# Last output projection of a two-block transformer kernel: first-half blocks without a barrier, second column half in two quarters

## The chip, the cores and the metric

One core of one Trainium2 chip. The metric is device time in microseconds (us) of one execution of the whole program; three executions of the kernel before took 3222.23, 3224.38 and 3224.39 us, median 3224.38. Engines: PE (TensorE, matmul) and PEld (its weight loads), DVE (VectorE), ACT (ScalarE), POOL (GpSimd), SP (SyncE, which issues the DMAs here).

## The reference

Two model blocks one after the other on x of 1024 tokens and 1024 channels, in float32. The first has a windowed attention mixer, a recurrent (LRU) mixer and two MLPs. The second, where the change lies, ends as follows (shortened):

```python
y_sb = stick_breaking_attention(...).reshape(B, S, SB_WIDTH) * jax.nn.silu(sb_g)
y_sw = sliding_window_sink_attention(...).reshape(B, S, SW_WIDTH) * jax.nn.silu(sw_g)
y = jnp.concatenate([y_sb, y_sw], axis=-1) @ w_out[l]
x = x + gate[:, None, :] * y
return rmsnorm(x, final_g)
```

So: an output projection 1024 x 1024, a gated residual, and an RMS norm over the channels of each token.

## The kernel before, in words

**Layout.** Activations lie transposed: channel n of a block of 128 on the partitions, tokens along the columns. X holds 8 such blocks of 128 x 1024. A "block" n of the output is 128 channels; "low" and "high" are the token columns 0 to 511 and 512 to 1023.

**Products in three parts.** Each float32 operand is split into a high part in fp32r (a copy by ACT) and the rest (a subtraction by DVE). A product is three matmuls: high x high, high x rest, rest x high. The activations' parts lie in H, the weights' in wsp.

**Weights.** `order` is a list written by hand of every weight block (128 x 1024, 512 KB) in the order of use. `load(b)` lets SP fetch block b into one of three buffers `raw`; `split(b)` has ACT copy it (wsp high) and DVE subtract (wsp rest), and then issues `load(b + 3)`. `piece(name)`, called as block b begins, splits blocks up to b + 2. The ACT copy of block b waits until TensorE is through with block b - 3.

**A projection.** `project` runs over output blocks: `take_pair` gives the next of four pairs of PSUM banks in turn, 8 x 3 matmuls of up to 512 columns go to it, and `evac` is called. The first matmul waits for `free` of both banks of the pair.

**The engines work in order.** `Queues.add` appends an instruction to one engine's list with the operations that it waits for; each engine works its list from the front. `Q.barrier()` puts a wait for the last operation of PE, ACT, DVE and POOL on each of these engines. Code lines of the profile are often a helper's: L283 `mm`, L138 `A` (an ACT activation), L141 `TT`, L144 `STT`, L149 `TS`, L415 the sum of squares in `Stats.add`, L399 the ACT table load, L66 a DMA issue.

**The end of the kernel.** The last attention (`attention_units` with `window_units`) has 16 units; between its steps TensorE gets pieces of other work in bank 7: eight gate jobs (`GateJob`) and the first four of the eight blocks of the out projection for the low columns (`OutJob`, in the order 0, 1, 6, 7). The attention also uses banks 0 to 6; its output of a unit leaves bank 6 by `out2`, whose parts go to H. `low_ready` names the operations that the low part of H depends on. `OutJob.leave` evacuates bank 7 by DVE (gated residual into X) and squares the result on ACT.

Then comes `Q.barrier()`, the ACT table load, and the loads of X blocks 2 to 5 from DRAM ("spill"), which wait for the barrier's operations. A first `project("out2", 4, ...)` computes the last four low blocks (2, 3, 4, 5), a second one the eight blocks of the high columns, 512 wide. `out_ev` evacuates a block: DVE adds gate x product to X, ACT squares it, DVE adds the square to a running sum (`Stats.add`; the first goes into the sum itself, the eighth into the total directly). After the second high block `root(0)` makes the low half's norm: `Stats.total` sums over the partitions on TensorE with a matrix of ones, then DVE, ACT (Ln, Exp) and three DVE operations (`finish`, `rsqrt`). From the fourth high block on each evacuation is followed by `final` of one low block: DVE multiplies X by the norm and SP writes 256 KB of output. After the last high block come the three low finals left, `root(1)` and eight finals of the high half.

```python
            for k in range(K):
                wh, wl, ready = piece(name)
...
                            op = mm(ps[:, c:c + m], w, r[:, c0 + c:c0 + c + m], k == 0 and i == 0, k == K - 1 and i == 2,
                                    ready, ops, *wait)
```

Of the kernel before, what the change touches and what calls it, by code (L numbers as in the profile page):

```python
# [10 lines left out]
ALU = mybir.AluOpType  # L11
# [102 lines left out]
def program(nc, D, out, stop=None, dbg=None):  # L114
    ctx = ExitStack()
    with ctx:
        def sb(name, shape, dt=F32):
            return ctx.enter_context(nc.sbuf_tensor(name, shape, dt))

        Q = Queues(nc, ctx)  # L120
# [10 lines left out]
        def dve(fn, *a):  # L131
            return Q.add("dve", fn, *a)
# [4 lines left out]
        def A(o, i, f, *a, **kw):  # L137
            return act(lambda e: e.activation(o, i, f, **kw), *a)  # L138
# [4 lines left out]
        def STT(o, x, s, y, op0, op1, *a):  # L143
            return dve(lambda e: e.scalar_tensor_tensor(out=o, in0=x, scalar=s, in1=y, op0=op0, op1=op1), *a)  # L144

        def TS(o, x, s1, s2, op0, op1, *a):
            if op1 is None:
                return dve(lambda e: e.tensor_scalar(o, x, s1, None, op0), *a)  # L148
            return dve(lambda e: e.tensor_scalar(o, x, s1, s2, op0, op1), *a)  # L149
# [4 lines left out]
        H = sb("H", [128, 2, 8, 1024], F32R)  # L154
# [13 lines left out]
        def place(off, shape, dt=F32):  # L168

            names[0] += 1  # L170
            with ExitStack() as st:
                if off:
                    st.enter_context(nc.sbuf_tensor(f"pad{names[0]}", [128, int(off) // 4], F32))
                return st.enter_context(nc.sbuf_tensor(f"p{names[0]}", shape, dt))

        def V(name, i=0, n=1):
            return vec[:, VEC[name] + i:VEC[name] + i + n]
# [7 lines left out]
        def blocks(name, idx, pieces=8):  # L185
            for i in idx:
                order.append((name, i, pieces))
# [29 lines left out]
        blocks("in2", (22, 23, 24, 25))  # L217
        blocks("in2", (22, 23, 24, 25))
        blocks("out2", (0, 1, 6, 7, 2, 3, 4, 5))
        blocks("out2", range(8))  # L220

        s_raw = [sem(f"s_raw{i}") for i in range(NR)]
# [23 lines left out]
        def piece(name):  # L246

            b, j = at
            assert order[b][0] == name, (order[b], name)
            if j == 0:  # L250
                for x in range(b + LA + 1):
                    split(x)
            return wsp[:, b % NS, 0, j * 128:(j + 1) * 128], wsp[:, b % NS, 1, j * 128:(j + 1) * 128], splits[b]

        def piece_done(op):
            b, j = at
            if j == order[b][2] - 1:
                uses[b] = [op]
                at[0], at[1] = b + 1, 0
            else:  # L260
                at[1] = j + 1
# [18 lines left out]
        X = place(0, [128, 8, 1024])  # L280

        def mm(o, l, r, start, stop, *a, **kw):
            return pe(lambda e: e.matmul(o, l, r, start=start, stop=stop, **kw), *a)  # L283
# [4 lines left out]
        def take_pair():  # L288
            p = pair[0]
            pair[0] = (p + 1) % 4  # L290
            return p

        def project(name, count, K, rhs, evac, N=1024, first=None, c0=0):
            later = first
            for n in range(count):
                p = take_pair()
                ps = PS[:, 2 * p:2 * p + 2, :].rearrange("p a b -> p (a b)")
                wait = [free[2 * p], free[2 * p + 1]]
                for k in range(K):
                    wh, wl, ready = piece(name)  # L300
                    rh, rl, ops = rhs(k)
                    for i, (w, r) in enumerate(((wh, rh), (wh, rl), (wl, rh))):
                        for c in range(0, N, 512):
                            m = min(512, N - c)
                            op = mm(ps[:, c:c + m], w, r[:, c0 + c:c0 + c + m], k == 0 and i == 0, k == K - 1 and i == 2,
                                    ready, ops, *wait)
                        wait = []
                    piece_done(op)
                if later:
                    later()  # L310
                fr, later = evac(n, p, ps[:, 0:N], op)
                free[2 * p] = free[2 * p + 1] = fr
            if later:
                later()
            return op
# [69 lines left out]
        Hops = [None] * 8  # L385
# [12 lines left out]
        def ln_exp():  # L398
            act(lambda e: e.preload_act_table_set("natural_log_exp_and_others"))  # L399
# [48 lines left out]
        def finish(st, R, M, y, t, N=1024):  # L448
            p, ps, o = st.total(N)
            m = TS(M, ps, 1.0 / 1024, eps_, ALU.mult, ALU.add, o)  # L450
            free[2 * p] = free[2 * p + 1] = [m]
            return rsqrt(R, y, t, M, m)
# [3 lines left out]
        def buf(off, N=1024):  # L456

            if (off, N) not in bufs:
                bufs[off, N] = place(off * KB, [128, N])
            return bufs[off, N][:, :]  # L460
# [161 lines left out]
        st = Stats(buf(80), [buf(84), buf(92)])  # L622
# [40 lines left out]
        for k in range(8):  # L663
            for j, p in enumerate(pairs):
                b = b0 + j
                rh, rl, ops = Hk(k)
                for i, (wi, r) in enumerate(((0, rh), (0, rl), (1, rh))):
                    for c in range(2):
                        op = mm(PS[:, 2 * p + c, :], wsp[:, b % NS, wi, k * 128:(k + 1) * 128], r[:, 512 * c:512 * c + 512],
                                k == 0 and i == 0, k == 7 and i == 2, splits[b], ops)  # L670
# [332 lines left out]
        ends = Q.barrier()  # L1003
# [29 lines left out]
        st = out_rest("out0", MOk, "mlp_norm0", xl0)  # L1033
# [6 lines left out]
        a = A(ct, V("c", 0, 8), ACT.Tanh, c_vec, scale=0.5)  # L1040
        o = STT(cond, ct, 1.0, V("c", 0, 8), ALU.add, ALU.mult, a)
# [142 lines left out]
        for n in range(8):  # L1184
# [23 lines left out]
            a = A(gq, gq, ACT.Tanh, L["gq"], scale=0.7978845608028654)  # L1208
# [12 lines left out]
        ends = Q.barrier()  # L1221
# [17 lines left out]
        st = out_rest("out1", MOk, "mlp_norm1", xl1)  # L1239
# [5 lines left out]
        o = STT(g2, modT[:, 8:16], 1.0, V("norm_g_2", 0, 8), ALU.add, ALU.mult, mod_ready)  # L1245
# [195 lines left out]
        for k in range(8):  # L1441
            o = STT(X[:, k, :], X[:, k, :], V("final_norm", k), R1, ALU.mult, ALU.mult, r1, Hops[k])
# [124 lines left out]
        for s in range(n_s + 3):  # L1567
# [17 lines left out]
            if 0 <= v < n_s:  # L1585
                c0, z, t, m, sh, sl, pb = view(v)
                o = A(m, m, ACT.Exp, F[v]["min"])
                o = A(m, m, ACT.Ln, o, bias=1.0)
                F[v]["m"] = STT(m, t, 0.125, m, ALU.mult, ALU.max, o)
            if s < n_s:  # L1590
                c0, z, t, m, sh, sl, pb = view(s)
                F[s]["zc"] = A(t, z, ACT.Copy, F[s]["qk"], got(s - 3, "pv"))
                free[ZB] = free[ZB + 1] = [F[s]["zc"]]
            if 0 <= u < n_s:
                c0, z, t, m, sh, sl, pb = view(u)
                F[u]["add"] = TT(t, t, pb, ALU.add, F[u]["cum"], F[u]["m"])
            if s < n_s:
                c0, z, t, m, sh, sl, pb = view(s)
                F[s]["min"] = TS(m, t, 0.125, 40.0, ALU.mult, ALU.min, F[s]["zc"], got(s - 2, "sl"), got(s - 2, "sh"))
            if 0 <= v < n_s:  # L1600
                c0, z, t, m, sh, sl, pb = view(v)
                F[v]["sh"] = A(sh, m, ACT.Copy, F[v]["m"], got(v - 2, "carry"))
                F[v]["sl"] = TT(sl, m, fz(sh), ALU.subtract, F[v]["sh"], got(v - 2, "carry"))
            if 0 <= u < n_s:
                c0, z, t, m, sh, sl, pb = view(u)
# [6 lines left out]
        ends = Q.barrier()  # L1612
# [10 lines left out]
        low, high = slice(0, 512), slice(512, 1024)  # L1623
        out_order = (0, 1, 6, 7, 2, 3, 4, 5)
        parts_of = [[None, None] for _ in range(8)]
        Hops[0:4] = [None] * 4
        st_low = Stats(buf(48)[:, low], [buf(52)[:, low], buf(52)[:, high]])
        st_high = Stats(buf(48)[:, high], [buf(96)[:, low], buf(96)[:, high]])
        after_gates = [None, None]

        class GateJob:
# [43 lines left out]
        def low_ready(k):  # L1675
            return parts_of[k][0] if k < 4 else [o for n in range(4) for o in parts_of[4 + n][0]]
# [31 lines left out]
        def left():  # L1708
            return bool(now["job"] or gates_left or outs_left)
# [41 lines left out]
                        dict(dve=ahead_dve, fill=ahead_fill, end=finish_now))  # L1751
        leave_now()
        assert not left() and not now["half"]
        ends = Q.barrier()
        ln_exp()
        for k in range(2, 6):
            xl3[k] = Q.dma(None, X[:, k, :], D["spill"][:, k, :], sp2[k], *ends)
        for f in sums:
            f()
        Hops[:] = [None] * 8  # L1760
        s_out = sem("s_out")
        fin = [dict(st=st_low), dict(st=st_high)]

        def root(hf):
            cs = slice(512 * hf, 512 * hf + 512)
            fin[hf]["r"] = finish(fin[hf]["st"], buf(72)[:, cs], buf(64)[:, cs], buf(76)[:, cs], buf(68)[:, cs], 512)

        def final(k, hf):
            x = X[:, k, 512 * hf:512 * hf + 512]
            o = STT(x, x, V("final_g_2", k), buf(72)[:, 512 * hf:512 * hf + 512], ALU.mult, ALU.mult, fin[hf]["r"])  # L1770
            return Q.dma(s_out, out[:, k, 512 * hf:512 * hf + 512], x, o)

        def out_ev(hf, at_n, x, p, ps, op):
            n = at_n[x]
            cs = (low, high)[hf]
            o = STT(X[:, n, cs], ps, modT[:, 16 + n:17 + n], X[:, n, cs], ALU.mult, ALU.add, op, xl3[n])
            fin[hf]["st"].add(8 - len(at_n) + x, X[:, n, cs], o)
            if hf and x == 1:
                root(0)
            if hf and x > 2:  # L1780
                final(x - 3, 0)
            return [o], None

        project("out2", 4, 8, Hk, lambda *a: out_ev(0, out_order[4:], *a), N=512)
        project("out2", 8, 8, Hk, lambda *a: out_ev(1, range(8), *a), N=512, c0=512)
        for k in range(5, 8):
            final(k, 0)
        root(1)
        for k in range(8):
            od = final(k, 1)  # L1790
        Q.add("sp", None, od, *sp1, *sp2, *mk_sp)
        assert at[0] == len(order), (at, len(order))
        block = ctx.enter_context(nc.Block())
# [128 lines left out]
```

How the kernel before makes its waits and increments, by code:

```python
            def run(eng):  # L93
                seen = {}
                for o in self.q[name]:
                    for d in o.deps:
                        if seen.get(d.sem.name, 0) < d.val:
                            eng.wait_ge(d.sem, d.val)
                            seen[d.sem.name] = d.val
                    if o.fn is None:
                        continue
                    ins = o.fn(eng)
                    if o.sem is not None:
                        ins.then_inc(o.sem, 1 if o.sem is self.sems.get(name) else 16)
```

## Time and profile before

| | |
|---|---|
| three executions | 3222.23, 3224.38, 3224.39 us |
| the profiled execution | 3220.72 us |
| its span, first to last instruction | 3218.9 us |
| mean granted TensorE clock | 0.987 |
| instructions | 34594 |
| HBM read, written | 170.63 MB, 14.68 MB |

The times in rows of the trace are microseconds from the start of the span, in the profiled execution. That execution is 3.66 us under the median of the three. A row of the timeline gives start, length, engine, line, operation, what it writes and reads, its size, and in brackets how long the engine stood idle before it and what ended that. The length of an instruction contains some latency: the next one on the same engine may start a little before its end.

### The profile page before, as it was taken

To read this page: it belongs to the slowest core of one execution; us is meant where nothing else is said; L and a number is where in the kernel's file an instruction comes from. 1 tells how busy PE (TensorE), PEld (TensorE's weight loads), DVE (VectorE), ACT (ScalarE), POOL (GpSimd) and SP (SyncE) were. 2 spreads that over 40 slices of the span, in tenths; PEclk is the share of its full clock that TensorE was granted. 3 is DMA by queue.
4 is the path that set the end of the run, shared out by engine and by line. 5 is a ranking of instruction groups with operands and counts; after the bars stand their busy time and mean duration, and the time that the engine had idled before them with its cause. 6 is when DMAs were issued, how large, how long until landed. Compare 5 with 4: busy or idle time off the path is not lost. (4 is left out here: it accounts for less than half of the span.)

```text
span 3218.9 us, 34594 instructions
## 1 busy us (share of the span) xinstructions
PE 3087.8 (96%) x14272; PEld 2391.5 (74%) x14272; DVE 1689.7 (52%) x2159; ACT 1099.7 (34%) x1711; POOL 89.9 (3%) x70
## 2 busy tenths in 40 slices
PE   8999999999999999999979999999999999999898
PEld 7884567788888888877767888888887686665566
DVE  7737854644444433589743633333334734566575
ACT  4215632311111111388622311111111515776452
POOL 0004510000000000000000000000000000000000
PEclk9999999999999999999989999999999999999999
DMA  4420011122222211211121111111111131000213
GB/s 148 116 90 1 1 73 40 58 68 72 71 66 78 73 46 53 75 47 43 59 85 40 45 48 46 46 51 48 46 46 46 53 124 33 20 20 14 92 53 111
DMA packets 53933, 188.86 MB, mean 59 GB/s; under 512 B 6224, under 2 KB 6608, under 8 KB 53648
## 3 DMA queue, kind: packets, MB, share of 16 engines
q1 hardware_dynamic: 53776, 186.65, 17.6%
q8 instruction: 113, 1.85, 0.2%
q14 instruction: 44, 0.36, 0.0%
HBM read 170.63 MB, written 14.68 MB: 58 GB/s over the span
## 5 line engine op out<-in xcount | busy, mean ns | idle before, releaser
L283 PE MATMUL PS<-H,wsp 128*128 128x512 f32 x6864 | 1612.0, 394 | 40.2 <-DVE wsp L141 17.0
L283 PEld LDWEIGHTS PS<-H,wsp 128*128 128x128 f32 x6864 | 1290.9, 189 | 344.9 <-issue 32.0
L283 PE MATMUL PS<-p,wsp 128*128 128x512 f32 (+1 forms) x3840 | 895.4, 393 | 20.7 <-DVE p L141 20.7
L283 PEld LDWEIGHTS PS<-p,wsp 128*128 128x128 f32 x3840 | 711.5, 189 | 198.6 <-ACT wsp L138 21.5
L138 ACT ACTIVATE p<-p 128x1024 f32<-128x1024 f32 (+7 forms) x426 | 361.0, 872 | 860.9 <-DVE p L144 680.0
L138 ACT ACTIVATE wsp<-raw 128x1024 fp32r<-128x1024 f32 (+1 forms) x263 | 272.6, 1040 | 703.4 <-PE PS L283 492.4
L141 DVE TENSOR_TENSOR p<-p,PS 128x1024 f32<-128x1024 f32 (+2 forms) x232 | 244.4, 1053 | 501.4 <-PE PS L283 501.2
L141 DVE TENSOR_TENSOR wsp<-raw,wsp 128x1024 fp32r<-128x1024 f32 (+1 forms) x263 | 316.9, 1207 | 162.0 <-ACT wsp L138 156.5
L141 DVE TENSOR_TENSOR p<-PS,p 128x1024 f32<-128x1024 f32 (+1 forms) x114 | 130.7, 1147 | 380.1 <-PE PS L283 355.9
L141 DVE TENSOR_TENSOR p<-p 128x1024 fp32r<-128x1024 f32 (+5 forms) x239 | 239.6, 1010 | 115.3 <-ACT p L138 112.1
L283 PE MATMUL PS<-p 128*64 128x256 f32 (+9 forms) x1432 | 284.9, 463 | 13.7 <-DMA p<-mk_dram 4.8
L144 DVE SCALAR_TENSOR_TENSOR p<-p 128x1024 f32<-128x1024 f32 (+3 forms) x197 | 209.5, 1070 | 68.4 <-ACT p L138 64.8
L138 ACT ACTIVATE p<-PS,sm 128x256 f32<-128x256 f32 (+2 forms) x256 | 127.9, 508 | 231.8 <-DVE sm L148 139.8
L138 ACT ACTIVATE p<-PS 128x512 f32<-128x512 f32 (+4 forms) x198 | 121.2, 639 | 221.7 <-PE PS L283 198.7
L283 PEld LDWEIGHTS PS<-p 128*64 128x64 f32 (+2 forms) x1432 | 123.8, 167 | 97.1 <-issue 55.4
L535 PE MATMUL PS<-cf,p 128*128 128x128 f32 x600 | 89.5, 284 | 23.4 <-DVE p L148 9.9
L498 DVE TENSOR_REDUCE sm<-PS 128x2 f32<-128x768 f32 (+3 forms) x96 | 94.7, 987 | 26.3 <-PE PS L283 25.9
L535 PEld LDWEIGHTS PS<-cf,p 128*128 128x128 f32 x600 | 67.2, 144 | 52.8 <-issue 14.9
L526 POOL TENSOR_SCALAR p<-p,sm 128x384 f32<-128x384 f32 (+1 forms) x64 | 87.8, 1373 | 250.2 <-DVE sm L519 250.2
L283 PE MATMUL PS<-p,triR 128*128 128x512 f32 (+3 forms) x352 | 79.4, 359 | 15.4 <-DVE p L141 14.6
L283 PE MATMUL PS<-wsp,H 128*128 128x256 f32 (+2 forms) x576 | 88.8, 316 | 0.0
L283 PEld LDWEIGHTS PS<-wsp,H 128*128 128x128 f32 x576 | 80.8, 190 | 7.8
(70 smaller groups left out, 1054.3 us busy)
## 6 DMA issues: line engine op xcount, KB each, us to landing
raw<-in_in_dram SPq DMA_DIRECT2D x70, 512.0 KB, 3.5
raw<-in_dn_dram SPq DMA_DIRECT2D x65, 512.0 KB, 3.5
raw<-in_up_dram SPq DMA_DIRECT2D x64, 512.0 KB, 3.5
raw<-in_out_dram SPq DMA_DIRECT2D x40, 512.0 KB, 3.5
p<-in_ada_dram SPq DMA_DIRECT2D x24, 512.0 KB, 4.4
p<-in_x_dram SPq DMA_DIRECT2D x16, 512.0 KB, 7.8
raw<-in_kv_dram SPq DMA_DIRECT2D x16, 512.0 KB, 3.5
spill_dram<-p SPq DMA_DIRECT2D x16, 512.0 KB, 3.0
```

What stands on the lines that cost most here:

```text
L138: return act(lambda e: e.activation(o, i, f, **kw), *a)
L141: return dve(lambda e: e.tensor_tensor(o, x, y, op), *a)
L144: return dve(lambda e: e.scalar_tensor_tensor(out=o, in0=x, scalar=s, in1=y, op0=op0, op1=op1), *a)
L283: return pe(lambda e: e.matmul(o, l, r, start=start, stop=stop, **kw), *a)
L498: o = dve(lambda e: e.tensor_reduce(mx, S, AX.X, ALU.max), op, prev)
L526: last[1] = pool(lambda e, P_=P_, r=r: e.tensor_scalar(P_, P_, r, None, ALU.mult), o)
L535: o = pe(lambda e, t_out=t_out, t_in=t_in: e.transpose(t_out, t_in, ident), probs[J * u + j], free[b])
```

## The change

The last projection's first-half blocks are issued with no barrier before them and wait for the parts of H (`low_ready`); the DMAs that waited on the barrier wait on the last operations of PE, ACT and DVE. The high half is computed in two passes over all eight weight blocks, for the columns 512 to 767 and 768 to 1023. The weight blocks of `out2` stand once more in `order`. There are three sets of column statistics, roots and finals: the low half (512 columns) and the two quarters (256 each). The root of a set is made after the second block of the next pass; its finals follow the fourth to eighth evacuation of that pass, in groups of 2, 2, 2, 1 and 1.

```diff
         blocks("out2", (0, 1, 6, 7, 2, 3, 4, 5))
+        blocks("out2", range(8))
         blocks("out2", range(8))
...
-        st_high = Stats(buf(48)[:, high], [buf(96)[:, low], buf(96)[:, high]])
+        spans = (low, slice(512, 768), slice(768, 1024))
+        st_high = [Stats(buf(48)[:, spans[1 + i]], [buf(96)[:, 512 * i + 256 * j:512 * i + 256 * j + 256] for j in range(2)])
+                   for i in range(2)]
...
-        ends = Q.barrier()
+        ends = [Q.last("pe"), Q.last("act"), Q.last("dve")]
         ln_exp()
         for k in range(2, 6):
             xl3[k] = Q.dma(None, X[:, k, :], D["spill"][:, k, :], sp2[k], *ends)
         for f in sums:
             f()
-        Hops[:] = [None] * 8
+        def high_ready(k):
+            return parts_of[k][1] if k < 4 else [o for n in range(4) for o in parts_of[4 + n][1]]
+
         s_out = sem("s_out")
-        fin = [dict(st=st_low), dict(st=st_high)]
...
+        fin = [dict(st=st) for st in (st_low, *st_high)]
+
+        def root(x):
+            cs = spans[x]
+            fin[x]["r"] = finish(fin[x]["st"], buf(72)[:, cs], buf(64)[:, cs], buf(76)[:, cs], buf(68)[:, cs],
+                                 cs.stop - cs.start)
+
+        def final(k, x):
+            cs = spans[x]
+            o = STT(X[:, k, cs], X[:, k, cs], V("final_g_2", k), buf(72)[:, cs], ALU.mult, ALU.mult, fin[x]["r"])
+            return Q.dma(s_out, out[:, k, cs], X[:, k, cs], o)
+
+        def out_ev(x, at_n, i, p, ps, op):
+            n, cs = at_n[i], spans[x]
             o = STT(X[:, n, cs], ps, modT[:, 16 + n:17 + n], X[:, n, cs], ALU.mult, ALU.add, op, xl3[n])
-            fin[hf]["st"].add(8 - len(at_n) + x, X[:, n, cs], o)
-            if hf and x == 1:
-                root(0)
-            if hf and x > 2:
-                final(x - 3, 0)
+            fin[x]["st"].add(8 - len(at_n) + i, X[:, n, cs], o)
+            if x and i == 1:
+                root(x - 1)
+            if x and i > 2:
+                for k in ((0, 1), (2, 3), (4, 5), (6,), (7,))[i - 3]:
+                    final(k, x - 1)
             return [o], None
 
-        project("out2", 4, 8, Hk, lambda *a: out_ev(0, out_order[4:], *a), N=512)
-        project("out2", 8, 8, Hk, lambda *a: out_ev(1, range(8), *a), N=512, c0=512)
-        for k in range(5, 8):
-            final(k, 0)
-        root(1)
+        project("out2", 4, 8, lambda k: (H[:, 0, k, :], H[:, 1, k, :], low_ready(k)),
+                lambda *a: out_ev(0, out_order[4:], *a), N=512)
+        for x in (1, 2):
+            project("out2", 8, 8, lambda k: (H[:, 0, k, :], H[:, 1, k, :], high_ready(k)),
+                    lambda *a: out_ev(x, range(8), *a), N=256, c0=spans[x].start)
+        root(2)
         for k in range(8):
-            od = final(k, 1)
+            od = final(k, 2)
```

## Rows read from the trace of the kernel before

**Rows 1.** The page: busy us, share of the span and instructions of each engine

```profile
PE 3087.8 (96%) x14272; PEld 2391.5 (74%) x14272; DVE 1689.7 (52%) x2159; ACT 1099.7 (34%) x1711; POOL 89.9 (3%) x70
```

**Rows 2.** The chain of waits, 3130 us to the end: start, length (us), what

```profile
3130.62 0.70 DVE p L144
...
3132.70 0.67 DVE p L144
...
3133.39 0.64 ACT p L138
...
3134.12 68.92 PE PS L283 x292
```

**Rows 3.** Timeline of TensorE, 3126 us to the end

```profile
3129.48 1.08 PE L283 MATMUL PS<-p 128*64 128x256 f32 x8
3134.12 34.50 PE L283 MATMUL PS<-H,wsp 128*128 128x512 f32 x144 [3.55 <-ACT p L138]
3168.46 1.88 PE L283 MATMUL PS<-p,cf 128*128 128x512 f32 x4
...
3204.62 1.96 PE L283 MATMUL PS<-p,cf 128*128 128x512 f32 x4 [1.60 <-ACT p L138]
```

**Rows 4.** Timeline of DVE and ACT in the last projection

```profile
3141.45 0.75 DVE L144 SCALAR_TENSOR_TENSOR p<-PS,modT,p 128x512 f32<-128x512 f32 x1 [3.75 <-PE PS L283]
...
3146.89 0.75 DVE L144 SCALAR_TENSOR_TENSOR p<-PS,modT,p 128x512 f32<-128x512 f32 x1 [1.81 <-PE PS L283]
3147.68 0.63 ACT L138 ACTIVATE p<-p 128x512 f32<-128x512 f32 x1 [3.86 <-DVE p L144]
3148.22 1.04 ACT L138 ACTIVATE wsp<-raw 128x1024 fp32r<-128x1024 f32 x1
...
3149.29 1.22 DVE L141 TENSOR_TENSOR wsp<-raw,wsp 128x1024 fp32r<-128x1024 f32 x1 [0.26 <-ACT wsp L138]
...
3157.77 0.75 DVE L144 SCALAR_TENSOR_TENSOR p<-PS,modT,p 128x512 f32<-128x512 f32 x1 [1.81 <-PE PS L283]
...
3174.83 1.22 DVE L141 TENSOR_TENSOR wsp<-raw,wsp 128x1024 fp32r<-128x1024 f32 x1
3175.97 0.74 DVE L144 SCALAR_TENSOR_TENSOR p<-PS,modT,p 128x512 f32<-128x512 f32 x1
```

**Rows 5.** TensorE's timeline, and windows: us, busy PE PEld DVE ACT POOL, PEclk, DMA, GB/s

```profile
3136.00:3138.00 2.00, 2.00 (x7) 1.59 (x6) 1.23 (x1) 0.45 (x1) 0.00 (x0) 0.61 0.98 393
...
3010.72 0.40 PE L283 MATMUL PS<-p,cb 128*128 128x128 bf16 x4 [1.84 <-ACT p L138]
...
3011.00:3013.00 2.00, 2.00 (x8) 1.58 (x7) 1.02 (x3) 0.93 (x5) 0.00 (x0) 0.57 0.57 141
...
3121.73 3.02 PE L283 MATMUL PS<-H,wsp 128*128 128x512 f32 x12 [1.66 <-DVE p L144]
...
3122.00:3123.00 1.00, 1.00 (x6) 0.78 (x6) 0.93 (x5) 1.00 (x3) 0.00 (x0) 1.00 0.00 0
```

**Rows 6.** Groups by shape on TensorE, columns 256: busy us, mean ns

```profile
L283 PE MATMUL PS<-p,wsp 128*128 128x256 f32 x192 | 23.4, 281 | 0.0
L283 PE MATMUL PS<-p,cf 128*128 128x256 f32 x4 | 1.0, 379 | 0.0
```

**Rows 7.** Groups by shape on DVE and ACT, 256 columns: busy us, mean ns

```profile
L144 DVE SCALAR_TENSOR_TENSOR p<-p 128x256 f32<-128x256 f32 x10 | 4.2, 422 | 4.0 <-ACT p L138 3.9
L144 DVE SCALAR_TENSOR_TENSOR p<-p,vec 128x256 f32<-128x256 f32 x8 | 3.8, 480 | 0.0
...
L138 ACT ACTIVATE p<-p 128x256 f32<-128x256 f32 x34 | 13.8, 411 | 10.7 <-DVE p L149 9.4 <-DVE p L415 0.9
```

**Rows 8.** Timeline of DVE: the eight final products at the end

```profile
3210.84 5.39 DVE L144 SCALAR_TENSOR_TENSOR p<-p,vec 128x512 f32<-128x512 f32 x8
```

**Rows 9.** DMA issues from 3100 us on: count, KB each, median us to landing

```profile
raw<-in_out_dram SPq DMA_DIRECT2D x10, 512.0 KB, 3.5
out_dram<-p SPq DMA_DIRECT2D x16, 256.0 KB, 2.1
```

More of the change, by code:

```diff
@@ L1759, in program @@
             f()
-        Hops[:] = [None] * 8
+        def high_ready(k):
+            return parts_of[k][1] if k < 4 else [o for n in range(4) for o in parts_of[4 + n][1]]
         s_out = sem("s_out")
-        fin = [dict(st=st_low), dict(st=st_high)]
[L1764 to L1771, printed above, removed]
@@ L1773, in out_ev @@
-        def out_ev(hf, at_n, x, p, ps, op):
-            n = at_n[x]
-            cs = (low, high)[hf]
-            o = STT(X[:, n, cs], ps, modT[:, 16 + n:17 + n], X[:, n, cs], ALU.mult, ALU.add, op, xl3[n])
-            fin[hf]["st"].add(8 - len(at_n) + x, X[:, n, cs], o)
-            if hf and x == 1:
-                root(0)
-            if hf and x > 2:
-                final(x - 3, 0)
-            return [o], None
-        project("out2", 4, 8, Hk, lambda *a: out_ev(0, out_order[4:], *a), N=512)
```

## The prediction

> **What bounds the kernel now.** I read the page first: TensorE's share of the span [rows 1]. TensorE is busy 96% of the time, so the only questions are where it stands still and how long the kernel runs after its last product. Next the chain of waits over the last 90 us [rows 2]. It goes through the last attention unit (DVE, ACT, DVE, DVE, ACT one after the other from 3130.62), then one unbroken piece of TensorE work of 68.92 us, then the tail: evacuation, square, column total, root, eight final products, output. Then TensorE's timeline of that stretch [rows 3]: it ends the attention at 3130.56, stands still 3.55 us, runs 144 products (four blocks of the first column half are 96, the rest are the second half) and a column total of 1.88 us; the last total starts after 1.6 us without work at 3204.62. Last, one step of DVE and ACT in this stretch [rows 4]: both have spare time, DVE's evacuation and subtraction take 2.0 us of a block of 5.44.
>
> So there are two places to gain, the gap at 3130.56 and the tail behind TensorE's piece, which ends at 3203.04 [rows 2]. TensorE's rate pays for everything between.
>
> **1. The barrier.** Without it the first block left (out2 number 4) needs its weights (split since 3123), its H parts (long done) and its PSUM pair. That last one decides. `take_pair` hands out the pairs in turn; counting its calls from the start of the program, 319 come before this block's, and 319 mod 4 is 3. Pair 3 is banks 6 and 7. Bank 7 is freed by the evacuation of the last block computed inside the attention, the DVE instruction that the chain shows from 3132.70 to 3133.37 [rows 2]. TensorE can start at about 3133.40 in place of 3134.12: **-0.72 us**, not 3.55. ACT's table load, the next weight copy and the spill loads that SP issues still wait for the square that ends at 3134.03. The new dependences of the spill loads name the same last operations, so they land as before. They are first needed when block 4 ends, after 3140, and are not late. No engine is queued behind anything new.
>
> **2. The clock.** After the 3.55 us gap the granted clock fell to half (1.2 GHz of 2.4); the first block's evacuation came 7.33 us after its start (3141.45) [rows 4], 1.7 over 5.44 and 0.17 of latency; the window of 3136 shows 0.61 [rows 5]. The new gap is 2.84 us. The trace has a shorter one that led to the same fall, 1.84 us before 3010.72 (granted clock 0.57 from 3011), while 1.66 us before 3121.73 did not (1.00 from 3122 on) [rows 5]. By these rows I keep the loss: 0. The Trainium skill, "TensorE: Matmul & The Clock Gate", section "HAM oscillation", asks for a gap longer than the new one before the clock drops; by it the clock would stay up here, and the 1.84 us row disagrees with it. By that rule the sum would be 1.7 us lower.
>
> **3. Products of half the width.** The second half is 8 blocks of 24 products of 512 columns, 5.44 us a block (evacuations at 3146.89 and, two blocks on, 3157.77 [rows 4]), 43.5 us. It becomes 16 blocks of 24 products of 256 columns. A group of 192 with this shape took 23.4 us [rows 6], 0.122 us each, 2.93 us a block, 46.8 us: **+3.3 us** at TensorE's pace. The column total of the first quarter is new on TensorE's queue: half of 1.88 us, **+0.95 us** (four narrow total products took 1.0 [rows 6]).
>
> **4. Weights twice.** Eight more blocks mean eight more SP loads of 512 KB, ACT copies of 1.05 us and DVE subtractions of 1.22 us. The block in front of them is now 2.93 us, not 5.44, and it is here that the cover goes. DVE and ACT work in order and wait for one another in a ring: evacuation (DVE), square (ACT), weight copy (ACT, queued behind the square), subtraction (DVE), next evacuation. At 512 columns the offsets are 0.79 to the square, 0.54 to the copy, 1.07 to the subtraction, and 1.14 from a subtraction to the next evacuation (3174.83 to 3175.97) [rows 4]: 3.54 us, well under 5.44. At 256 columns, with 0.48 for an operation with a vector operand, 0.42 without, 0.41 on ACT [rows 7], 0.03 for a handover, and 0.06 to 0.08 less between independent neighbours (products 0.75 long stand 0.67 apart [rows 8]): 0.51 + 0.33 + 1.08 + 1.14 = **3.06 us, over TensorE's 2.93**. With the other work DVE has in a step:
> - two 512-wide final products (0.67 each, eight took 5.39): 0.95 to the sum of squares, 0.36 for it, 1.35, 1.14 = 3.80 us, three steps; with one, 3.12, and once, beside the last block, 3.06;
> - the 512-wide root: 1.31, 0.72, ACT 0.66 + 0.66, DVE 0.72 + 0.72 + 0.69, 1.14 = 6.62 us;
> - the 256-wide root: 1.31, 0.45, 0.44 + 0.44, 0.46 + 0.45 + 0.42, 1.14 = 5.11 us;
> - two 256-wide final products (0.42 each): 3.29 us.
>
> The look-ahead of two blocks hides some of the lag, then it is used up. From the last evacuation of the first half, 3157.77 - 0.72 = 3157.05: 3.54 + 3.06 + 6.62 + 3.06 + 3 x 3.80 + 3.12 + 3.06 (first quarter), + 3.06 + 5.11 + 3.06 + 2 x 3.29 (second, to its sixth evacuation) = 3208.7. From there on DVE has no weights left to split: 3.29 - 1.14, then 0.95 + 0.36 + 0.42 (one final left in front) put the last evacuation at **3212.6**. TensorE, which could begin its last block when the last subtraction ended at 3208.8, is through at 3212.0, a little sooner. Against 3203.07: **+9.5 us**. By TensorE's pace alone it would be -0.72 + 3.3 + 0.95 = +3.5; the other 6 us is DVE's lag.
>
> **5. The tail.** Before, the last evacuation starts 0.03 us behind TensorE's piece, at 3203.07, and the eighth final product ends at 3216.23 [rows 8]: 13.16 us. At 256 columns: evacuation 0.51, square 0.44, total 1.08, mean 0.45, two ACT steps 0.88, three DVE steps 1.36, eight finals 7 x 0.42 + 0.48 = 8.1, with the small waits 8.2: **-5.0 us**. The last write is 128 KB, not 256; it lands 2.1 us after issue now [rows 9]. The new one I put 0.3 us sooner; bounds 0 and 0.8, what a write that starts before the engines are full could save.
>
> **Sum:** +9.5 - 5.0 - 0.3 = **+4.2 us**. The profiled execution took 3220.72 us, its span 3218.9, so 3224.9 on its scale. It is 3.7 under the median of the runs, and I add the change to the median: 3224.38 + 4.2 = 3228.6, written as **3228.5**.
>
> **Loads.** A raw buffer is loaded after its subtraction and wanted by the copy three blocks on, about 7 us later at the new rhythm; landing takes 3.5 us [rows 9]. Final writes of 512 KB a step now run beside them, together about 300 GB/s; the window of 3136 shows 393 GB/s [rows 5]. I cost it at 0. The cover is gone if landing passes 7 us.
>
> **The rivals.**
> A, the forecast: DVE's ring sets the pace of both quarters. Own range 3226.5 to 3231, chance 0.50.
> B, the same, but the granted clock does not fall after the shorter gap: -1.7, 3226.8. For it: the gap shrank by a fifth. Against it: the 1.84 us row. Chance 0.15. (The rule of the Trainium skill named under 2 points to this one.)
> C, DVE keeps up (the square and the copy overlap more than in rows 4, or narrow operations are cheaper than rows 7), TensorE sets the pace: +3.5 - 5.0 - 0.3 = -1.8, 3222.6. Against it: DVE's own work in a step with two finals is 0.42 + 0.36 + 1.35 + 1.14 = 3.3, over 2.93 with no wait at all. Chance 0.12.
> D, slower: weight loads come late. Its place is the stretch in which first-quarter finals, 256 KB each, go out between weight loads on the one SP queue. It decides from a landing time of 7 us; at 9 us three-block cycles last 9 + 2.3 in place of some 10, and over the quarters 4.6 us are added (3233.1), at 10 us 7.6 (3236). For it: writes and loads share the DMA engines, and in the window of 3136 these are full (share 0.98) [rows 5]. Chance 0.18.
> E, the bank is another and TensorE starts at 3130.6: -2.8 on A, with the clock kept -4.5, 3224.0 to 3225.7. That is the change doing what it says in full. Chance 0.05.
>
> **How the numbers follow.** 0.2% is 6.4 us, about what a measurement of this kernel can tell from no change. Faster by more needs C and E together with the clock kept (-1.8 - 2.8 - 1.7 = -6.3), and the error of the medians on top: 0.03. Slower by more: D, and the top of A if the clock also falls once at the narrow root: 0.24. The rest, 0.73, is within. Range: from C, 3222.5, to the lower part of D, 3233.5.
>
> **What would show it.** Right: TensorE's restart after the attention about 0.7 us sooner with an idle time of 2.8 us; matmuls of 256 columns at 0.122 us each; TensorE idle on DVE's weight subtraction, 4 to 6 us in all, in the stretch from about 3170; DVE without idle time on TensorE there; last evacuation near 3212.6; tail of 8.2 us. Wrong: a restart near 3130.6, no TensorE idle time behind the subtraction (C), or idle time in front of ACT's weight copy, ended by a load (D). A time under 3220 or over 3236 would break the whole account.

## The result, and the profile after

The changed kernel took 3228.71 us in the median of 19 executions, the kernel before 3222.23 us in 19 beside them. The two medians are 6.5 us apart, 0.20%. The ratio with its interval, 1.0015 with 95% within 1.0008 to 1.0022, puts the change lower: 2.6 to 7.1 us slower, 4.8 at the middle (the means of the 19 are 4.7 apart). The forecast was +4.2 us.

The two profiled executions differ by more, 3218.9 and 3227.0 us. 3.7 us of that lie ahead of anything the change touches: the last attention product ends at 3130.57 in the one and 3134.24 in the other, with the same instructions up to there and the granted clock falling at other places (from 86 to 94 us, for one, it is 1.00 before and 0.79 in the changed kernel). So the traces are compared from the end of the last attention product on. I call the time from there to the end of the span the **stretch**: 88.3 us before, 92.7 us after, **+4.4 us**.

Engine totals on the page of the changed kernel hardly show it: 9 us more on TensorE, 12 on DVE.

```profile
span 3227.0 us, 35088 instructions
...
PE 3097.1 (96%) x14468; PEld 2406.5 (75%) x14468; DVE 1702.1 (53%) x2193; ACT 1108.5 (34%) x1729; POOL 89.7 (3%) x70
```

TensorE's timeline answers to [rows 3].

```profile
3133.16 1.08 PE L284 MATMUL PS<-p 128*64 128x256 f32 x8
3137.18 29.39 PE L284 MATMUL PS<-H,wsp 128*128 128x512 f32 x144 [2.94 <-DVE p L144]
3166.40 1.88 PE L284 MATMUL PS<-p,cf 128*128 128x512 f32 x4
3167.72 6.31 PE L284 MATMUL PS<-H,wsp 128*128 128x256 f32 x48
3174.23 6.16 PE L284 MATMUL PS<-H,wsp 128*128 128x256 f32 x48 [0.20 <-DVE wsp L141]
3181.05 3.11 PE L284 MATMUL PS<-H,wsp 128*128 128x256 f32 x24 [0.66 <-DVE wsp L141]
...
3202.86 12.62 PE L284 MATMUL PS<-H,wsp 128*128 128x256 f32 x96 [1.45 <-DVE wsp L141]
3217.01 1.10 PE L284 MATMUL PS<-p,cf 128*128 128x256 f32 x4 [1.53 <-ACT p L138]
```

Before, TensorE stood still 3.55 us for ACT, which came through the barrier; now it stands still 2.94 us for one DVE instruction, the evacuation of bank 7. And inside the quarters there is idle time that the kernel before did not have: five waits for DVE's weight subtraction. The view of the waits from 3135 on sums TensorE's (us in total, times, longest):

```profile
PE PS L284 <- DVE wsp L141: 3.6, 5, 1.5
PE PS L284 <- DVE p L144: 2.9, 1, 2.9
PE PS L284 <- ACT p L138: 1.5, 1, 1.5
```

The ring of DVE and ACT, timeline of both, to set beside [rows 4]: one plain step from 3174.00, then one with two finals from 3177.06.

```profile
3174.00 0.48 DVE L144 SCALAR_TENSOR_TENSOR p<-PS,modT,p 128x256 f32<-128x256 f32 x1
...
3174.51 0.42 ACT L138 ACTIVATE p<-p 128x256 f32<-128x256 f32 x1 [2.79 <-DVE p L144]
3174.83 1.05 ACT L138 ACTIVATE wsp<-raw 128x1024 fp32r<-128x1024 f32 x1
3174.96 0.42 DVE L416 TENSOR_TENSOR p<-p 128x256 f32<-128x256 f32 x1 [0.49 <-ACT p L138]
3175.91 1.23 DVE L141 TENSOR_TENSOR wsp<-raw,wsp 128x1024 fp32r<-128x1024 f32 x1 [0.53 <-ACT wsp L138]
3177.06 0.48 DVE L144 SCALAR_TENSOR_TENSOR p<-PS,modT,p 128x256 f32<-128x256 f32 x1
...
3178.36 1.41 DVE L144 SCALAR_TENSOR_TENSOR p<-p,vec 128x512 f32<-128x512 f32 x2
...
3179.69 1.22 DVE L141 TENSOR_TENSOR wsp<-raw,wsp 128x1024 fp32r<-128x1024 f32 x1
3180.82 0.48 DVE L144 SCALAR_TENSOR_TENSOR p<-PS,modT,p 128x256 f32<-128x256 f32 x1
```

The plain step is 3.06 us (3174.00 to 3177.06), the other 3.76. No evacuation here has idle time of DVE in front of it that a TensorE product ended: TensorE's results are ready, and it is DVE that is late. In the plain step DVE itself is idle for 0.49 and 0.53 us, both times for ACT. That is the ring.

The end of the kernel, DVE's timeline (compare [rows 8]) and the DMA issues from 3160 on (compare [rows 9]):

```profile
3215.94 0.48 DVE L144 SCALAR_TENSOR_TENSOR p<-PS,modT,p 128x256 f32<-128x256 f32 x1
...
3220.89 3.26 DVE L144 SCALAR_TENSOR_TENSOR p<-p,vec 128x256 f32<-128x256 f32 x8
```

```profile
raw<-in_out_dram SPq DMA_DIRECT2D x11, 512.0 KB, 3.6
out_dram<-p SPq DMA_DIRECT2D x8, 256.0 KB, 2.8
out_dram<-p SPq DMA_DIRECT2D x16, 128.0 KB, 1.8
```

### The profile page after: what moved, and what is told of

It reads as the page before. It is cut to its first block and busy times, and to the rows that moved or that the text cites. A ratio compares the mean times of both kernels' runs of the same rounds, so it can differ in the third digit from the quotient of the medians.

```text
span 3227.0 us, 35088 instructions
## 1 busy us (share of the span) xinstructions
PE 3097.1 (96%) x14468; PEld 2406.5 (75%) x14468; DVE 1702.1 (53%) x2193; ACT 1108.5 (34%) x1729; POOL 89.7 (3%) x70
## 5 line engine op out<-in xcount | busy, mean ns | idle before, releaser
L284 PE MATMUL PS<-H,wsp 128*128 128x512 f32 (+1 forms) x7056 | 1619.5, 389 | 43.1 <-DVE wsp L141 20.1
L138 ACT ACTIVATE wsp<-raw 128x1024 fp32r<-128x1024 f32 (+1 forms) x271 | 280.9, 1040 | 705.0 <-PE PS L284 492.4
L141 DVE TENSOR_TENSOR wsp<-raw,wsp 128x1024 fp32r<-128x1024 f32 (+1 forms) x271 | 326.6, 1207 | 164.6 <-ACT wsp L138 159.2
L527 POOL TENSOR_SCALAR p<-p,sm 128x384 f32<-128x384 f32 (+1 forms) x64 | 87.7, 1371 | 251.2 <-DVE sm L520 251.2
```

Of the source, the lines that this page charges most:

```text
L141: return dve(lambda e: e.tensor_tensor(o, x, y, op), *a)
L527: last[1] = pool(lambda e, P_=P_, r=r: e.tensor_scalar(P_, P_, r, None, ALU.mult), o)
```

## The experiments

The theory is the forecast's: bank 7 holds back the restart, and in the quarters the order of work in the queues of DVE and ACT, not TensorE, sets the pace. The rivals are the full gain of the barrier, late loads, and the price of narrow products. Every kernel was profiled; where a ratio stands, it was also timed over 11 executions (the changed kernel over 19) beside the kernel before. Rows with one execution rest on their trace alone. The columns that I compare:

| kernel | idle before restart | last evacuation | stretch | ratio to before (95%) |
|---|---|---|---|---|
| before | 3.55 | 72.5 | 88.3 | |
| changed | 2.94 | 81.7 | 92.7 | 1.0015 (1.0008 to 1.0022) |
| barrier_only | 2.94 | 71.9 | 87.7 | 0.9999 (0.999 to 1.0008) |
| quarters_only | 3.55 | 82.2 | 93.2 | 1.0012 (1.0003 to 1.0021) |
| after_next_pair | none | 77.1 | 88.1 | 1.0002 (0.9993 to 1.0012) |
| after_no_sub | 2.94 | 75.3 | 86.3 | one execution |
| width_only | 3.55 | 75.0 | 90.8 | one execution |
| after_ring_open | 2.94 | 75.2 | 86.3 | one execution |
| halves_next_pair | none | 67.4 | 83.1 | 0.9982 (0.9973 to 0.9991) |
| ring_open_next_pair | none | 70.7 | 81.7 | 0.9982 (0.9973 to 0.9992) |

Times in us; the last evacuation is counted, like the stretch, from the end of the last attention product. "None" means that TensorE's row there shows no idle time.

**barrier_only** takes one part of the change alone.

```diff
-        ends = Q.barrier()
+        ends = [Q.last("pe"), Q.last("act"), Q.last("dve")]
...
-        project("out2", 4, 8, Hk, ...)
-        project("out2", 8, 8, Hk, ..., N=512, c0=512)
+        project("out2", 4, 8, lambda k: (H[:, 0, k, :], H[:, 1, k, :], low_ready(k)), ...)
+        project("out2", 8, 8, lambda k: (H[:, 0, k, :], H[:, 1, k, :], high_ready(k)), ..., N=512, c0=512)
```

> The kernel before with the barrier alone taken out (blocks wait for their parts of H), the second half still 512 wide. The stretch counted is from the end of the last attention product to the end of the span: 88.3 us before, 92.8 us in the changed kernel. Theory (the first block left waits for bank 7): TensorE stands still 2.9 us in place of 3.55, the stretch is 87.7, and the time is 0.6 us lower, which no median can show. Rival (the barrier was worth its whole gap): idle time under 0.3 us and a stretch of 84.8 or less.

Stretch 87.7, as the theory has it; TensorE's timeline names the same waited-for instruction as in the changed kernel:

```profile
3124.77 1.08 PE L283 MATMUL PS<-p 128*64 128x256 f32 x8
3128.79 34.51 PE L283 MATMUL PS<-H,wsp 128*128 128x512 f32 x144 [2.94 <-DVE p L144]
```

The barrier was worth 0.6 us, because another wait ended 0.6 us before it. That is read from the traces; the ratio can't tell 0.6 us from nothing.

**quarters_only** is the changed kernel with the barrier back (the first two lines above, the other way round).

> The changed kernel with the barrier put back: the two quarters alone. Theory: all of the loss is the quarters'; stretch 93.4 us (92.8 + 0.6), time 5 us over the kernel before. Rival (taking out the barrier let other work collide and made part of the loss): stretch under 92.8.

93.2, and a ratio clear of 1. The two parts add: -0.6 and +4.9 make the change's 4.4 to within 0.1. The quarters are the whole loss.

**after_next_pair** tests that it is the bank.

```diff
+        take_pair()
         project("out2", 4, 8, lambda k: (H[:, 0, k, :], H[:, 1, k, :], low_ready(k)),
```

> The changed kernel with one pair of banks skipped ahead of the remaining first-half blocks, so that the first of them gets banks 0 and 1 and the fourth gets 6 and 7. Theory: TensorE goes on without standing still (under 0.3 us in place of 2.94), the granted clock stays at full, the first block takes 5.6 us to its evacuation instead of 7.35, and the stretch falls from 92.8 by 2.9 + 1.7 = 4.6 to 88.2, level with the kernel before. The first evacuation can be late by a spill load that lands after it. Rival (another wait stands right behind the bank, the spill loads or the weight split): idle time stays over 2 us and the stretch over 91. Second rival (DVE sets the pace so firmly that the earlier start is lost again): evacuations of the quarters come no earlier than in the changed kernel, counted from the end of the attention.

```profile
3128.84 1.08 PE L284 MATMUL PS<-p 128*64 128x256 f32 x8
3129.86 27.84 PE L284 MATMUL PS<-H,wsp 128*128 128x512 f32 x144
3157.54 1.88 PE L284 MATMUL PS<-p,cf 128*128 128x512 f32 x4
```

No idle time, and 144 products take 27.84 us in place of 29.39. The granted clock (the value after the five engines in the window rows) is 1.00 after the restart here and fell to 0.50, the lower level, in the changed kernel:

```profile
3139.00:3141.00 2.00, 2.00 (x6) 1.58 (x5) 0.90 (x1) 1.06 (x1) 0.00 (x0) 0.50 0.82 285
...
3130.00:3140.00 10.00, 10.00 (x44) 8.22 (x45) 5.79 (x8) 5.19 (x6) 0.00 (x0) 1.00 0.56 204
```

The stretch is 88.1 for 88.2 expected; the last evacuation moved by 4.6 us, the same amount as the restart and the clock together, so the second rival falls too. One skipped pair is worth seven times what the removed barrier was. The first block's evacuation came at 7.3 us after the attention, not 5.6, which the expectation had allowed for: the block needs X from a spill load, which now lands later than the product and a weight subtraction that stands ahead of it on DVE (3135.79 to 3137.02; the last 0.18 us before the evacuation at 3137.19 are a wait for that load). The second block's came at 11.2 all the same; TensorE's row above has no idle time from it.

**after_no_sub** takes DVE's work away.

```diff
             o1 = A(h, src, ACT.Copy, loads[b], uses.get(b - NS), splits.get(b - NS))
-            o2 = TT(l, src, fz(h), ALU.subtract, o1, uses.get(b - NS), loads[b], splits.get(b - NS))
+            if b >= len(order) - 16:
+                o2 = o1
+            else:
+                o2 = TT(l, src, fz(h), ALU.subtract, o1, uses.get(b - NS), loads[b], splits.get(b - NS))
```

> The changed kernel without the DVE subtraction that makes the low part of the weights, for the last 16 blocks of weights (both quarters); it leaves out that part of the computation, and the products with the low part read what an earlier block left there. Theory (the ring of DVE and ACT sets the pace): with 1.22 us less on DVE in each step TensorE sets the pace again; its idle time on weights in the quarters goes from 3.6 us to 0, evacuations stand 2.95 us apart, and the last evacuation, 81.7 us after the end of the attention in the changed kernel and 72.5 in the one before, comes at about 76 (72.5 + 3.3 + 0.95 - 0.6). Rival (loads of weights or the width of the products set the pace): last evacuation stays over 80.

TensorE's wait for weights is gone, and the quarters run in unbroken pieces:

```profile
3167.18 23.59 PE L287 MATMUL PS<-H,wsp 128*128 128x256 f32 x192
3190.62 1.02 PE L287 MATMUL PS<-p,cf 128*128 128x256 f32 x4
3191.29 17.62 PE L287 MATMUL PS<-H,wsp 128*128 128x256 f32 x144
```

The last evacuation comes at 75.3 (76 expected), and with DVE free the evacuations stand 2.88 us apart. All widths are as in the changed kernel, so they did not set its pace. The loads are the same in number and size, but not in time: a raw buffer is free here after the copy, without waiting for a subtraction, so its next load can go out sooner. That late loads were not the cause is shown by the changed kernel's own trace, in which no weight copy of the last projection waits for a load. DVE set the pace; but whether by how much it has to do or by its order this run can't tell.

**after_ring_open** takes nothing away. `split` is cut in two, and `out_ev` hands the next weight copy to ACT ahead of the square, and the subtraction to DVE ahead of the sum of squares and the root; the finals come ahead of the subtraction.

```diff
...
             o = STT(X[:, n, cs], ps, modT[:, 16 + n:17 + n], X[:, n, cs], ALU.mult, ALU.add, op, xl3[n])
-            fin[x]["st"].add(8 - len(at_n) + i, X[:, n, cs], o)
-            if x and i == 1:
-                root(x - 1)
+            nb = at[0] + LA
+            c = split_high(nb)
             if x and i > 2:
                 for k in ((0, 1), (2, 3), (4, 5), (6,), (7,))[i - 3]:
                     final(k, x - 1)
+            split(nb, c)
+            fin[x]["st"].add(8 - len(at_n) + i, X[:, n, cs], o)
+            if x and i == 1:
+                root(x - 1)
             return [o], None
```

> The changed kernel with the opened ring alone (no pair skipped). Theory: gap of 2.9 us and half clock as in the changed kernel, last evacuation at about 75.3 us after the end of the attention (as in the run without the subtraction) in place of 81.7, stretch 86.3 in place of 92.7. Rival (the ring is only part of the lag): last evacuation over 78.

TensorE's timeline has no wait for weights left:

```profile
3163.30 23.59 PE L292 MATMUL PS<-H,wsp 128*128 128x256 f32 x192
...
3187.41 17.62 PE L292 MATMUL PS<-H,wsp 128*128 128x256 f32 x144
```

Last evacuation at 75.2, the same as without the subtraction (75.3): 6.5 us came back by order alone. The edit moves the copy, the subtraction and the finals together; what each move is worth was not tried. The rival that DVE has too much work is wrong on the whole, though it does fall behind in the steps with two 512-wide finals. DVE's timeline of such a step, in ring_open_next_pair, which has the same order:

```profile
3170.43 0.48 DVE L144 SCALAR_TENSOR_TENSOR p<-PS,modT,p 128x256 f32<-128x256 f32 x1
3170.82 1.41 DVE L144 SCALAR_TENSOR_TENSOR p<-p,vec 128x512 f32<-128x512 f32 x2
3172.14 1.22 DVE L141 TENSOR_TENSOR wsp<-raw,wsp 128x1024 fp32r<-128x1024 f32 x1
3173.28 0.42 DVE L424 TENSOR_TENSOR p<-p 128x256 f32<-128x256 f32 x1
3173.61 0.48 DVE L144 SCALAR_TENSOR_TENSOR p<-PS,modT,p 128x256 f32<-128x256 f32 x1
```

3.18 us a step with no idle time, 0.3 over TensorE's 2.88, in three steps; the look-ahead of two blocks covers that. In the changed kernel the same work took 3.76.

**width_only** is the kernel before with each weight tile in wsp used for two products of 256 columns in place of one of 512.

```diff
...
-                        for c in range(0, N, 512):
-                            m = min(512, N - c)
-                            op = mm(ps[:, c:c + m], w, r[:, c0 + c:c0 + c + m], k == 0 and i == 0, k == K - 1 and i == 2,
+                        for c in range(0, N, 256 if two else 512):
+                            m = min(256 if two else 512, N - c)
+                            op = mm(PS[:, 2 * p + c // 256, 0:256] if two else ps[:, c:c + m], w,
+                                    r[:, c0 + c:c0 + c + m], k == 0 and i == 0, k == K - 1 and i == 2,
```

> The kernel before with the second half's products cut to 256 columns, two beside each other for each weight tile, in the two banks of the pair; every weight block is still used once. It measures the width alone. From the run without the subtraction: 2.88 us for 24 narrow products, so 5.76 a block in place of 5.44 and 5.34, the last evacuation 2.6 to 3.4 us later than 72.5, at 75.5, and the stretch 91.3. Rival (narrow products cost more only when each brings new weights): under 73.5. With the barrier in place, gap 3.55 us.

Blocks of the second half stand 5.76 us apart, twice 2.88, and the last evacuation is 2.5 us later than before. So narrow products cost the same whether or not each weight block is fetched and split for its 256 columns alone. What the run does not separate is the load of the tile into TensorE: that still goes with every product, 487 loads by the rows in place of 288.

```profile
L283 PEld LDWEIGHTS PS<-H,wsp 128*128 128x128 f32 x487 | 66.8, 194 | 9.0 <-issue 4.5
```

Whether the extra time is that of the loads or of the shorter products stays open. The 2.5 us are the plain price of the narrow products on TensorE. The new column total adds 0.85: in the run without the subtraction, the two blocks around it end 6.61 us apart (3190.82 to 3197.43), where 5.76 are products. That is 3.4 us in all.

**halves_next_pair** and **ring_open_next_pair** ask what of it beats both kernels. The first is barrier_only with `take_pair()`; the second is after_ring_open with `take_pair()`.

> The kernel before without the barrier, with one pair of banks skipped ahead of the remaining first-half blocks; the second half 512 wide in one pass. If gap, clock and quarters simply add: the stretch from the end of the last attention product to the end of the span is 87.7 (barrier alone out) less the 2.9 us gap and the 1.6 us of half clock = 83.1 us, 5.2 under the kernel before. Rival (the earlier start is given back where the spill loads or the tail end last): 86 or more.

> The changed kernel with the skipped pair, and with the ring of DVE and ACT opened: after each evacuation the next weight copy comes ahead of the square on ACT, and the subtraction ahead of the sum of squares and the root on DVE. No operation is added or left out. Theory (it is the order in the two queues, not DVE's amount of work, that makes the quarters slow): TensorE waits for weights 0.3 us at most in place of 3.6, evacuations come 2.88 us apart, the last one 70.7 us after the end of the attention in place of 77.1, and the stretch is 81.8 us against 88.1 with the skipped pair alone. Rival (DVE has too much to do in the steps with two 512-wide finals, 3.3 us of its own work in 2.9): TensorE still waits 2 us or more and the stretch stays over 84.

Both come out as added up, 83.1 and 81.7, and both are faster than the kernel before, ratio 0.9982, with intervals that end under 1. TensorE's waits in ring_open_next_pair from 3130 on are a single row, the square before the last column total:

```profile
PE PS L292 <- ACT p L138: 1.1, 1, 1.1
```

By the traces the quarters with the ring open are 1.4 us ahead of the halves: 3.3 us more up to the last evacuation, 4.7 us less from there to the end. The timed medians (3216.43 and 3217.93 us) agree in sign, but the two intervals are nearly the same, so the times don't show it.

The next limit is already to be seen there. The view of the tile raw in ring_open_next_pair, from 3160 on, has the weight copy waiting for loads, which happened nowhere in the last projection of the changed kernel:

```profile
  DMA raw<-in_out_dram: 5.1, 4
...
DMA to landing us min/median/max: 3.4/4.4/5.8
```

TensorE did not feel it yet.

## Why the prediction was right, point by point

The change and its mechanism were right; that the time itself, 3228.5 us, came within 0.2 us of 3228.71 is luck. The forecast stood on a median of three executions, 3224.38; over 19 the kernel before has 3222.23, and the 2.15 us too many there made up for the 2.3 us by which the two medians differ by more than +4.2.

**1, the barrier.** -0.72 us forecast, -0.6 measured in barrier_only, and by the wait that was named. From the evacuation's end to the restart 0.03 us was put, and in the changed kernel it is 0.14 (3137.04 to 3137.18). The counted pair was the right one: skipping it removed the gap.

**2, the clock.** Kept as a loss, and it stayed one: after the 2.94 us gap the granted clock fell in the changed kernel, barrier_only, after_no_sub and after_ring_open, each time with the first evacuation 10.3 us after the attention. In the three kernels that closed the gap it did not fall (1.00 over the ten microseconds after the restart), which is worth 1.6 us (forecast 1.7). By the Trainium skill, "TensorE: Matmul & The Clock Gate", section "HAM oscillation", a gap of this length should not have cost the clock; four traces of four, with 2.94 us each, say it does here.

**3, half the width.** 2.93 us a block forecast, 2.88 measured; +3.3 became +2.5, and the column total's +0.95 became +0.85. By TensorE's pace alone the last evacuation would thus be 2.8 us later, not 3.5 (75.3 against 72.5 without the subtraction). The error does not show in the time, because DVE's ring set the pace: the lag of 6 us came out as 6.5.

**4, the ring.** Forecast steps against the changed kernel's trace: plain 3.06 and 3.06, with the wide root 6.62 and 6.55, two wide finals 3.80 and 3.76, the narrow root 5.11 and 5.06, two narrow finals 3.29 and 3.23. Last evacuation +9.5 forecast, +9.2 measured. TensorE's waits for the subtraction sum to 3.6 us, a little under the 4 to 6 that were named as the sign. The lag was the main term, and after_no_sub and after_ring_open show its cause from two sides: take the work away or change its order, and it goes.

**5, the tail.** From the last evacuation to the end of the last product 8.2 forecast, 8.21 measured (3215.94 to 3224.15), against 13.16: -5.0.

**The output was mis-sized.** I put its end 0.3 us sooner; it came 0.2 us later. From the last product to the end of the span it was 2.67 us before and is 2.85 now. The write does land sooner, 1.8 us after its issue in place of 2.1. But it is issued late. The view of the output writes, the last eight of the changed kernel:

```profile
L66 SPq DMA_DIRECT2D out_dram<-p x8: 332/450/453, 3221.4 to 3224.7; - x8
```

and of the kernel before:

```profile
L66 SPq DMA_DIRECT2D out_dram<-p x8: 332/332/332, 3211.6 to 3216.3; - x8
```

An issue takes SP 0.45 us in the median here and took 0.33 before; eight of them start 0.47 apart, while DVE delivers a product every 0.40. The last issue begins 0.57 us after the last product's end (3224.72 against 3224.15), before it began as the product ended (3216.26 and 3216.23). The forecast put nothing for SP's issues.

**The sum.** The barrier's -0.6 is already in the last evacuation: +9.2 - 4.95 + 0.2 = +4.4 in the trace, 4.8 (2.6 to 7.1) in the times, +4.2 forecast.

**The rivals.** C, that DVE keeps up, fell with 3.6 us of waits for the subtraction. It describes after_ring_open, where DVE does keep up: stretch 86.3, 2.0 under the kernel before, where C had -1.8. D, late loads, fell: landing took 3.6 us in the median and 5.6 at most, under the 7 us from which it would decide, and no copy waited for a load. B fell with the clock. E fell with the 2.94 us gap, and after_next_pair, which is E made on purpose, gave -4.6 against the -4.5 put down for it.

## What to carry to other kernels

Before a barrier is taken out, look for the wait that ends next: here a PSUM bank, handed out in turn, ended 0.6 us earlier, and moving on by one pair gave 4.6 us where removing the barrier gave 0.6. When a step on the busiest engine is halved, write down the loop through the in-order queues of the engines that serve it, not their busy time: DVE at 2.0 of 5.44 us looked idle, but its loop with ACT was 3.06 us long and the new step 2.88. Here the loop was opened by order alone, with the operations that feed the bounding engine ahead of the bookkeeping.

## What was not expected

- How much of the delay was order and how little was work: 6.5 us of the 9.2 (81.7 to 75.2) came back with every instruction still there.
- Inside the attention TensorE stands still for 1.85 us and, some 80 us later, for about 1.65 us, the same in every profile. In six of the ten the clock fell after the first and not after the second, in the other four after the second and not after the first: 12 products behind it took 4.6 us in place of 3.0. Which of the two it is was not explained. The falls go with the time: of 27 executions of the kernel before, from 3212.5 to 3225.5 us, the shortest has a mean granted clock of 0.989 and the three longest 0.985. This is why the stretch was compared and not the span.
- SP's issues of the last eight 128 KB writes, in a row, took 0.45 us each; those of 256 KB, further apart, 0.33. It is not the size: the eight 128 KB writes before them, not in one row, took 0.34 in the median. Why the closer ones take longer was not tried.
